# A mixture-of-experts loop whose blocks are pipelined by one: the down matmuls of a block between the gate-and-up chunks of the next

## The chip, the cores and the metric

The kernel runs on one core of a Trainium2 chip (trn2). The metric is the device time of one execution in microseconds. Times of before are of three runs and one profiled execution.

## The reference, cut to what matters

One step of an encoder layer on 336 tokens (64 of a sample stream, 272 of a prompt stream), all in fp32: norm and input projection, an mLSTM branch, a latent-attention branch, output projection, then a top-4-of-32 mixture of experts with clamped SwiGLU, and a final norm. The change touches the mixture of experts alone:

```python
logits = (x2 @ w_router) + b_router
top_v, top_i = lax.top_k(logits, 4)
gates = softmax(top_v)
...
def expert_block(xb, e):
    gu = xb @ w_gu[e] + b_gu[e]            # 1024 x 2048
    gate = minimum(gu[:, :1024], 7.0)
    up = clip(gu[:, 1024:], -7.0, 7.0)
    hid = (up + 1.0) * gate * sigmoid(1.702 * gate)
    return hid @ w_dn[e] + b_dn[e]         # 1024 x 1024
...
y[token] += expert_block(x2[token], e) * gate
```

## The kernel before, in words

The kernel is one program with an instruction stream written out by hand for each engine (sync, tensor, scalar, vector, gpsimd); engines meet at semaphores, and each stream runs in its own order. A long first part computes the mixing branches and the router. The change lies behind it, in the expert loop.

**Blocks.** Each token goes to four experts. The 1344 token rows are sorted by expert and padded to blocks of 64 rows (`BLK`). Every expert has at least one block. The number of blocks, `nb`, is read from a table at run time, as are the expert of each block (`bei`) and, for each expert, the last block of the expert before it (`firsti`). GpSimd scatters the normed rows into a DRAM buffer `x_rows` by an indirect DMA, and gathers the results from `y_rows` afterwards.

**Weights.** An expert has 8 MB of gate-and-up weights and 4 MB of down weights. The SBUF buffer `ring` has six slots of 2 MB: chunks 0 to 3 hold gate-and-up (two of eight contraction tiles each, `up_w`), chunks 4 and 5 hold down (`dn_w(0)`, `dn_w(1)`). Each chunk has one slot, so chunk c of an expert is loaded into the slot that the same chunk of the expert before has left. SyncE issues these loads in one stream:

```python
with sp.Fori(1, NE) as e:
    before = sp.value_load(firsti[...e...])
    for c in range(4):
        sp.wait_ge(m_up, before * 4 + c + 1)
        sp.dma_start(up_w(c), ...).then_inc(chunk_in[c], 16)
    for c in range(2):
        sp.wait_ge(m_down, before * 2 + c + 1)
        sp.dma_start(dn_w(c), ...).then_inc(chunk_in[4 + c], 16)
```

The waits are on the last block of the expert before. Lines 473 to 482; the change leaves them as they are. Chunks of expert 0 are loaded ahead of the loop.

**One block on TensorE** (lines 809 to 854): four bias matmuls (line 817) with a selection matrix `pick`; gate-and-up chunks 0 to 2 (line 826) and chunk 3 (line 834), gate half first, then up half; the eight turnings (transposes, line 502 by the helper `turn`) of the next block's token rows, `tokens_turned`; the four turnings of the hidden rows; the down matmuls in two halves (line 851). Bias and gate-and-up accumulate in banks 2 and 3, turned rows stand in banks 0 and 1, down in bank 4. The two column halves of a matmul go to two halves of the array's columns, so matmuls stand in pairs.

**Beside it.** VectorE clamps gate and up out of the banks (lines 1422, 1425; helper line 1112), makes `pick` for the next block, and multiplies (1428, 1430). ScalarE applies the sigmoid (1070), copies the turned tokens to `xg` (1072), the turned hidden rows to `hidT` (1074) and the result to `yrow` (1077); copies show as line 878. GpSimd loads the next block's rows into the one buffer `xrow` (1517), stores `yrow` in two halves (1521) and waits for the stores before it goes on (1522).

Of the kernel before, what the change touches and what calls it, by code (L numbers as in the profile page):

```python
# [15 lines left out]
F32 = mybir.dt.float32  # L16
# [6 lines left out]
D = 1024  # L23
# [133 lines left out]
def build(nc, i, o, x_rows_dram, y_rows_dram):  # L157
    with ExitStack() as ctx:
# [3 lines left out]
        def sem(name):  # L162
            return ctx.enter_context(nc.semaphore(name))
# [156 lines left out]
        def taken(eng, *name):  # L320
# [21 lines left out]
             "m_dve", "m_pick", "m_turn", "m_hidT", "fin_v", "fin_ss", "fin_s", "fin_out", "all_out"))  # L342
        m_rows_in = sem("m_rows_in")
        desti_set, blocks_out, x_sent = sem("desti_set"), sem("blocks_out"), sem("x_sent")
# [141 lines left out]
        def _(pe):  # L486
# [321 lines left out]
            tokens_turned()  # L808
            with pe.Fori(0, nb) as b:
                e = pe.value_load(bei[0:1, bass.ds(b, 1)].bitcast(I32), min_val=0, max_val=NE - 1)  # L810

                def half(bank, t):
                    return bank[BLK * t:BLK * t + BLK, :]

                pe.wait_ge(m_pick, b + 1)
                for q in range(4):
                    pe.matmul(half(gate_bank if q < 2 else up_bank, q % 2), pick[:, q, :], bgu[:, :],  # L817
                              start=True, stop=False, skip_group_check=True)
                pe.wait_ge(m_xg, b + 1)
                for c in range(4):  # L820
                    pe.wait_ge(chunk_in[c], 16 * e + 16)
                    w = up_w(c)
                    if c < 3:
                        for k in range(2):
                            for q in range(4):
                                ins = pe.matmul(half(gate_bank if q < 2 else up_bank, q % 2), xg[:, 2 * c + k, :],  # L826
                                                w[:, k, 512 * q:512 * q + 512], start=False, stop=False,
                                                skip_group_check=True)
                        ins.then_inc(m_up, 1)
                    else:  # L830
                        for bank_, q0, done in ((gate_bank, 0, m_gate), (up_bank, 2, m_up)):
                            for k in range(2):
                                for t in range(2):
                                    ins = pe.matmul(half(bank_, t), xg[:, 2 * c + k, :],  # L834
                                                    w[:, k, 512 * (q0 + t):512 * (q0 + t) + 512], start=False,
                                                    stop=(k == 1), skip_group_check=True)
                            ins.then_inc(done, 1)
                pe.wait_ge(m_xrow, 16 * b + 32)
                pe.sem_inc(m_rows_in, 1)
                tokens_turned()  # L840
                pe.wait_ge(m_hid, b + 1)
                for j in range(4):
                    ins = turn(ht_bank[:, 128 * j:128 * j + 128], hid[:, 128 * j:128 * j + 128])
                ins.then_inc(m_turn, 1)
                pe.wait_ge(m_hidT, b + 1)
                for c in range(2):
                    pe.wait_ge(chunk_in[4 + c], 16 * e + 16)
                    w = dn_w(c)
                    for j in range(4):
                        for t in range(2):  # L850
                            ins = pe.matmul(half(out_bank, t), hidT[:, j, BLK * c:BLK * c + BLK],  # L851
                                            w[:, j, 512 * t:512 * t + 512], start=(c == 0 and j == 0),
                                            stop=(c == 1 and j == 3), skip_group_check=True)
                    ins.then_inc(m_down, 1)


        @block.scalar
        def _(act):
# [208 lines left out]
            signal(tokens(), m_xg, 1)  # L1067
            with act.Fori(0, nb) as b:
                act.wait_ge(m_gt, b + 1)
                act.activation(sg, gt, ACT.Sigmoid, scale=ALPHA).then_inc(m_sig, 1)  # L1070
                act.wait_ge(m_gath, b + 2)
                tokens().then_inc(m_xg, 1)
                act.wait_ge(m_turn, b + 1)
                copy(hidT[:, :, :], banks[1][:, :].rearrange("p (j s) -> p j s", j=4)).then_inc(m_hidT, 1)
                act.wait_ge(m_down, 2 * b + 2)
                act.wait_ge(yrow_free, b + 1)
                copy(yrow, banks[4][:, :]).then_inc(m_yrow, 1)
                act.wait_ge(m_yrow, b + 1)
                act.wait_ge(moe_tab, 1)
                act.nop()  # L1080


# [9 lines left out]
        def _(dve):  # L1092
# [327 lines left out]
            with dve.Fori(0, nb) as b:  # L1420
                dve.wait_ge(m_gate, b + 1)
                ts(gt, banks[2][:, :], LIMIT, ALU.min).then_inc(m_gt, 1)
                ts(pick[:, :, :], lane, be[:, bass.ds(dve.snap(b + 1), 1)], ALU.is_equal).then_inc(m_pick, 1)
                dve.wait_ge(m_up, 4 * b + 4)
                ts(up, banks[3][:, :], LIMIT, ALU.min, -LIMIT, ALU.max).then_inc(m_dve, 1)
                dve.wait_ge(m_sig, b + 1)
                dve.wait_ge(m_gt, b + 1)
                tt(gt, gt, sg, ALU.mult).then_inc(m_dve, 1)
                dve.wait_ge(m_dve, 2 * b + 2)
                stt(hid, up, 1.0, gt, ALU.add, ALU.mult).then_inc(m_hid, 1)  # L1430
                dve.wait_ge(m_hid, b + 1)
                dve.wait_ge(m_pick, b + 2)
                dve.wait_ge(moe_tab, 1)
                dve.nop()
# [20 lines left out]
        def _(pool):  # L1455
# [10 lines left out]
            for n in range(16):  # L1466
                b0, b1 = (MAXB + 1) * n // 16, (MAXB + 1) * (n + 1) // 16
                pool.dma_start(x_rows_dram[b0 * BLK:b1 * BLK, :].rearrange("(b s) d -> s b d", s=BLK),
# [43 lines left out]
            pool.sem_inc(yrow_free, 1)  # L1512
            with pool.Fori(0, nb) as b:
                src = x_rows_dram[bass.ds(pool.snap(b * BLK + BLK), BLK), :]
                dst = y_rows_dram[bass.ds(pool.snap(b * BLK), BLK), :]
                pool.wait_ge(m_gath, b + 1)
                pool.dma_start(xrow, src).then_inc(m_xrow, 16)
                pool.wait_ge(m_yrow, b + 1)
                pool.wait_ge(moe_tab, 1)
                for h in range(2):  # L1520
                    pool.dma_start(dst[:, 512 * h:512 * h + 512], yrow[BLK * h:BLK * h + BLK, :]).then_inc(m_store, 16)  # L1521
                pool.wait_ge(m_store, 32 * b + 32)
                pool.sem_inc(yrow_free, 1)
            pool.wait_ge(m_store, 32 * nb)
            pool.wait_ge(m_xrow, 16 * nb + 16)
            word = u_pad[0:1, 0, 67:68]
# [50 lines left out]
```

## Time and profile before

| | us |
|---|---|
| median of 3 runs (lowest to highest) | 2060.36 (2055.08 to 2061.68) |
| profiled execution, own time | 2061.79 |
| its span, first to last instruction | 2060.2 |
| TensorE matmul busy | 1719.9 (83%) |
| VectorE, ScalarE, GpSimd busy | 372.7, 337.3, 117.5 |
| mean granted TensorE clock | 0.887 of full speed |

Spans and starts are counted from the profile's first instruction; each engine's busy time is the union of its instructions. "PE" is TensorE, "DVE" VectorE, "ACT" ScalarE, "POOL" GpSimd, "SP" SyncE; a q behind an engine is its sequencer. A timeline merges like instructions in a row: start, us, engine, line, operation, output and inputs, how many, and in brackets the idle time before them with what ended it. A matmul of an fp32 operand stands as two instructions, so a chunk of 8 matmuls shows as x16.

### The profile page before, as it was taken

Reading aid. Unit: us, or ns where it says so; the run is one execution under the profiler, and the core shown is the slowest. Engines: PE = TensorE matmul, PEld = TensorE weight load, DVE = VectorE, ACT = ScalarE, POOL = GpSimd, SP = SyncE. Lnnn points to the kernel's source line nnn. Section 1 sums busy time; section 2 is a strip of 40 time slices with the busy share of each in tenths; the row PEclk is TensorE's granted clock in tenths of the full one; section 3 lists DMA queues with packets and bytes.
Section 4 is the critical chain, followed back from the end, with each engine's and each line's share of the span. In section 5 each row is a group of like instructions: output and inputs, shape, how many; then the busy total and the mean of one; then the engine's idle time right before and its main releaser. Section 6 shows DMA issues by size and latency. Waiting matters only on the chain.

```text
span 2060.2 us, 19415 instructions
## 1 busy us (share of the span) xinstructions
PE 1719.9 (83%) x7088; PEld 789.1 (38%) x7089; DVE 372.7 (18%) x899; ACT 337.3 (16%) x695; POOL 117.5 (6%) x219
## 2 busy tenths in 40 slices
PE   3999978688889998589877999979799987899890
PEld 1666544355556663333222333323233322233330
DVE  1371143322220011511010111101110111011113
ACT  1141254211221000111110111101111110111111
POOL 0021000000000000200000000000000000000003
PEclk9999976766669999599999999998999999999995
DMA  9396200110013344399999879999977999759894
GB/s 306 118 256 196 102 21 0 34 39 2 1 41 123 113 169 156 141 367 405 408 405 402 317 272 403 405 403 413 401 297 267 412 402 399 290 209 403 315 365 137
DMA packets 112324, 510.75 MB, mean 248 GB/s; under 512 B 8513, under 2 KB 12334, under 8 KB 79390
## 3 DMA queue, kind: packets, MB, share of 16 engines
q1 hardware_dynamic: 95790, 454.97, 56.4%
q0 software_dynamic: 16496, 55.29, 9.2%
q8 instruction: 22, 0.36, 0.1%
q14 instruction: 16, 0.13, 0.0%
HBM read 470.95 MB, written 39.28 MB: 248 GB/s over the span
## 4 chain that ended last, share of the span: by engine, by line
PE 65%; DMA 22%; DVE 6%; ACT 3%; issue 3%; SPq 1%; POOL 0%; DVEq 0%; POOLq 0%; ACTq 0%
PE bank L498 31%; DMA ring<-in_w_gate_up 18%; PE bank L826 12%; PE bank L851 10%; PE bank L834 7%; PE bank L502 2%; PE bank L817 2%; DVE r_c L1118 1%; DMA ring<-in_w_down 1%; ACT ring L878 1%; DMA ring<-in_w_in 1%; DVE r_v L1118 1%; DVE r_kv L1115 1%; ACT r_kv L878 1%; DMA y_rows<-r_xt 0%
## 5 line engine op out<-in xcount | busy, mean ns | idle before, releaser
L826 PE MATMUL bank<-ring,r_kv 128*64 128x512 f32 x1872 | 412.9, 593 | 27.2 <-DMA ring<-in_w_gate_up 27.2
L851 PE MATMUL bank<-ring,r_kv 128*64 128x512 f32 x1248 | 315.0, 662 | 27.8 <-ACT r_kv L878 26.8
L498 PE MATMUL bank<-r_xt,ring 128*128 128x336 f32 (+2 forms) x896 | 259.8, 453 | 8.6 <-DMA ring<-in_w_in 8.6
L826 PEld LDWEIGHTS bank<-ring,r_kv 128*64 128x64 f32 x1872 | 131.2, 137 | 302.6 <-issue 253.4
L1112 DVE TENSOR_SCALAR r_kv<-bank 128x512 f32<-128x512 f32 (+1 forms) x80 | 55.0, 687 | 1038.0 <-PE bank L834 1016.2
L498 PEld LDWEIGHTS bank<-r_xt,ring 128*128 128x128 f32 (+2 forms) x896 | 167.5, 188 | 99.1 <-issue 20.4
L834 PE MATMUL bank<-ring,r_kv 128*64 128x512 f32 x624 | 151.3, 630 | 39.9 <-DMA ring<-in_w_gate_up 39.9
L851 PEld LDWEIGHTS bank<-ring,r_kv 128*64 128x64 f32 x1248 | 94.7, 153 | 223.2 <-issue 181.5
L1070 ACT ACTIVATE r_o<-r_kv 128x512 f32<-128x512 f32 x39 | 24.6, 630 | 562.2 <-DVE r_kv L1112 562.2
L502 PE MATMUL bank<-const,r_v 64*128 64x64 f32 (+3 forms) x524 | 62.9, 258 | 60.0 <-DVE r_v L1118 49.3
L834 PEld LDWEIGHTS bank<-ring,r_kv 128*64 128x64 f32 x624 | 45.5, 144 | 141.6 <-issue 88.4
L498 PE MATMUL bank<-ring 64*128 64x257 f32 (+4 forms) x208 | 78.6, 526 | 22.4 <-DVE r_qk L1115 11.1
L1521 POOL DMA_DIRECT2D y_rows<-r_xt x78 | 41.8, 536 | 855.0 <-ACT r_xt L878 833.7
L502 PEld LDWEIGHTS bank<-const,r_v 64*128 64x128 f32 (+3 forms) x524 | 46.2, 140 | 100.2 <-DVE r_v L1118 54.5
L878 ACT ACTIVATE r_xt<-bank 128x512 f32<-128x512 f32 x39 | 23.3, 597 | 320.0 <-PE bank L851 320.0
L817 PE MATMUL bank<-bgu,r_qk 128*64 128x512 f32 x312 | 74.8, 601 | 0.0
L498 PE MATMUL bank<-r_kv,ring 128*128 128x336 f32 (+10 forms) x240 | 73.8, 448 | 0.0
L878 ACT ACTIVATE r_kv<-bank 128x512 f32<-128x512 f32 (+3 forms) x85 | 49.8, 586 | 134.8 <-PE bank L502 134.6
L498 PEld LDWEIGHTS bank<-ring 64*128 64x128 f32 (+4 forms) x208 | 42.9, 223 | 52.5 <-issue 34.0
L498 PEld LDWEIGHTS bank<-r_kv,ring 128*128 128x128 f32 (+3 forms) x240 | 44.7, 225 | 26.1 <-issue 15.5
L498 PE MATMUL bank<-ring,r_kv 128*128 128x128 f32 (+4 forms) x160 | 49.1, 453 | 6.4 <-ACT ring L878 6.4
L1070 ACT ACT_TABLE_LOAD x39 | 50.0, 1283 | 12.7 <-ACT r_xt L878 12.6
(212 smaller groups left out, 1092.7 us busy)
## 6 DMA issues: line engine op xcount, KB each, us to landing
ring<-in_w_gate_up SPq DMA_DIRECT2D x128, 2048.0 KB, 20.6
ring<-in_w_down SPq DMA_DIRECT2D x64, 2048.0 KB, 21.4
ring<-in_w_in SPq DMA_DIRECT2D x12, 2048.0 KB, 7.8
r_v<-x_rows POOLq DMA_DIRECT2D x40, 256.0 KB, 7.3
y_rows<-r_xt POOLq DMA_DIRECT2D x78, 128.0 KB, 5.5
x_rows<-r_c POOLq DMA_DIRECT2D x10, 768.0 KB, 18.4
x_rows<-r_c POOLq DMA_DIRECT2D x6, 1024.0 KB, 21.6
y_rows<-r_c POOLq DMA_DIRECT2D x1, 5376.0 KB, 33.1
```

Of the source, the lines that this page charges most:

```text
L498: ins = pe.matmul(out, l, r, start=(n == 0), stop=(n == len(pairs) - 1), **kw)
L502: return pe.transpose(out, src, ident[0:src.shape[0], 0:src.shape[0]])
L817: pe.matmul(half(gate_bank if q < 2 else up_bank, q % 2), pick[:, q, :], bgu[:, :], start=True, stop=False, skip_group_check=True)
L826: ins = pe.matmul(half(gate_bank if q < 2 else up_bank, q % 2), xg[:, 2 * c + k, :], w[:, k, 512 * q:512 * q + 512], start=False, stop=Fal ...
L834: ins = pe.matmul(half(bank_, t), xg[:, 2 * c + k, :], w[:, k, 512 * (q0 + t):512 * (q0 + t) + 512], start=False, stop=(k == 1), skip_grou ...
L851: ins = pe.matmul(half(out_bank, t), hidT[:, j, BLK * c:BLK * c + BLK], w[:, j, 512 * t:512 * t + 512], start=(c == 0 and j == 0), stop=(c ...
L878: return act.activation(out, src, ACT.Copy, scale=scale)
L1070: act.activation(sg, gt, ACT.Sigmoid, scale=ALPHA).then_inc(m_sig, 1)
L1112: return dve.tensor_scalar(out, a, s1, s2, op0, op1)
L1115: return dve.tensor_tensor(out, a, b, op)
L1118: return dve.scalar_tensor_tensor(out=out, in0=a, scalar=s, in1=b, op0=op0, op1=op1)
L1521: pool.dma_start(dst[:, 512 * h:512 * h + 512], yrow[BLK * h:BLK * h + BLK, :]).then_inc(m_store, 16)
```

## The change

The TensorE stream is cut into `bias`, `gate_up`, `hidden_turned` and `down`. Block 0's bias and gate-and-up run ahead of the loop; each iteration then does bias and chunk 0 of block b, the hidden turning of block b-1, chunk 1, the down matmuls of block b-1, chunks 2 and 3 and the turning of the next token rows; the last block's down stands behind the loop. A new semaphore `m_read` says that the up half has been read, and the bias of the next block waits for it. `down` waits for `yrow_free`, where the ScalarE copy did before. ScalarE's hidden and result copies move by one block to the head of its iteration. GpSimd issues the row load of block b+2 in iteration b, behind the stores of block b-1, and `x_rows` gets one more zeroed block. The body of `gate_up` is the old one, indented otherwise, as is that of `half`.

```diff
-        m_rows_in = sem("m_rows_in")
+        m_rows_in, m_read = sem("m_rows_in"), sem("m_read")
...
@@ -806,43 +806,48 @@
-            with pe.Fori(0, nb) as b:
-                e = pe.value_load(bei[0:1, bass.ds(b, 1)].bitcast(I32), min_val=0, max_val=NE - 1)
...
+            def bias(b):
 
                 pe.wait_ge(m_pick, b + 1)
                 for q in range(4):
                     pe.matmul(half(gate_bank if q < 2 else up_bank, q % 2), pick[:, q, :], bgu[:, :],
                               start=True, stop=False, skip_group_check=True)
-                pe.wait_ge(m_xg, b + 1)
-                for c in range(4):
-                    pe.wait_ge(chunk_in[c], 16 * e + 16)
-                    w = up_w(c)
-                    if c < 3:
+
+            def gate_up(c, e):
+
+                pe.wait_ge(chunk_in[c], 16 * e + 16)
+                w = up_w(c)
+                if c < 3:
...
-                pe.wait_ge(m_xrow, 16 * b + 32)
-                pe.sem_inc(m_rows_in, 1)
-                tokens_turned()
...
+            def hidden_turned(b):
+
                 pe.wait_ge(m_hid, b + 1)
                 for j in range(4):
                     ins = turn(ht_bank[:, 128 * j:128 * j + 128], hid[:, 128 * j:128 * j + 128])
                 ins.then_inc(m_turn, 1)
+
+            def down(b, e):
+
                 pe.wait_ge(m_hidT, b + 1)
+                pe.wait_ge(yrow_free, b + 1)
...
+            bias(0)
+            pe.wait_ge(m_xg, 1)
+            for c in range(4):
+                gate_up(c, 0)
+            pe.wait_ge(m_xrow, 32)
+            tokens_turned()
+            with pe.Fori(1, nb) as b:
+                e = pe.value_load(bei[0:1, bass.ds(b, 1)].bitcast(I32), min_val=0, max_val=NE - 1)
+                before = pe.value_load(bei[0:1, bass.ds(pe.snap(b - 1), 1)].bitcast(I32), min_val=0, max_val=NE - 1)
+                pe.wait_ge(m_read, b)
+                bias(b)
+                pe.wait_ge(m_xg, b + 1)
+                gate_up(0, e)
+                hidden_turned(b - 1)
+                gate_up(1, e)
+                down(b - 1, before)
+                gate_up(2, e)
+                gate_up(3, e)
+                pe.wait_ge(m_xrow, 16 * b + 32)
+                pe.sem_inc(m_rows_in, 1)
+                tokens_turned()
+            hidden_turned(nb - 1)
+            down(nb - 1, NE - 1)
...
@@ -1065,19 +1094,30 @@
-            with act.Fori(0, nb) as b:
+
+            def hidden_out(b):
+                act.wait_ge(m_turn, b + 1)
+                copy(hidT[:, :, :], banks[1][:, :].rearrange("p (j s) -> p j s", j=4)).then_inc(m_hidT, 1)
+
+            def rows_out(b):
+                act.wait_ge(m_down, 2 * b + 2)
+                copy(yrow, banks[4][:, :]).then_inc(m_yrow, 1)
+
+            act.wait_ge(m_gt, 1)
+            act.activation(sg, gt, ACT.Sigmoid, scale=ALPHA).then_inc(m_sig, 1)
+            act.wait_ge(m_gath, 2)
+            tokens().then_inc(m_xg, 1)
+            with act.Fori(1, nb) as b:
+                hidden_out(b - 1)
+                rows_out(b - 1)
                 act.wait_ge(m_gt, b + 1)
                 act.activation(sg, gt, ACT.Sigmoid, scale=ALPHA).then_inc(m_sig, 1)
                 act.wait_ge(m_gath, b + 2)
                 tokens().then_inc(m_xg, 1)
-                act.wait_ge(m_turn, b + 1)
-                copy(hidT[:, :, :], banks[1][:, :].rearrange("p (j s) -> p j s", j=4)).then_inc(m_hidT, 1)
-                act.wait_ge(m_down, 2 * b + 2)
-                act.wait_ge(yrow_free, b + 1)
-                copy(yrow, banks[4][:, :]).then_inc(m_yrow, 1)
-                act.wait_ge(m_yrow, b + 1)
                 act.wait_ge(moe_tab, 1)
                 act.nop()
+            hidden_out(nb - 1)
+            rows_out(nb - 1)
...
@@ -1422,11 +1462,12 @@
-                ts(up, banks[3][:, :], LIMIT, ALU.min, -LIMIT, ALU.max).then_inc(m_dve, 1)
+                ts(up, banks[3][:, :], LIMIT, ALU.min, -LIMIT, ALU.max).then_inc(m_read, 1)
...
-                dve.wait_ge(m_dve, 2 * b + 2)
+                dve.wait_ge(m_read, b + 1)
+                dve.wait_ge(m_dve, b + 1)
...
@@ -1464,7 +1505,7 @@
-                b0, b1 = (MAXB + 1) * n // 16, (MAXB + 1) * (n + 1) // 16
+                b0, b1 = (MAXB + 2) * n // 16, (MAXB + 2) * (n + 1) // 16
...
@@ -1510,19 +1551,27 @@
-            with pool.Fori(0, nb) as b:
-                src = x_rows_dram[bass.ds(pool.snap(b * BLK + BLK), BLK), :]
-                dst = y_rows_dram[bass.ds(pool.snap(b * BLK), BLK), :]
-                pool.wait_ge(m_gath, b + 1)
-                pool.dma_start(xrow, src).then_inc(m_xrow, 16)
-                pool.wait_ge(m_yrow, b + 1)
+            pool.wait_ge(m_gath, 1)
+            pool.dma_start(xrow, x_rows_dram[BLK:2 * BLK, :]).then_inc(m_xrow, 16)
+            pool.wait_ge(m_gath, 2)
+            pool.dma_start(xrow, x_rows_dram[2 * BLK:3 * BLK, :]).then_inc(m_xrow, 16)
+            with pool.Fori(1, nb) as b:
+                src = x_rows_dram[bass.ds(pool.snap(b * BLK + 2 * BLK), BLK), :]
+                dst = y_rows_dram[bass.ds(pool.snap(b * BLK - BLK), BLK), :]
+                pool.wait_ge(m_yrow, b)
                 pool.wait_ge(moe_tab, 1)
                 for h in range(2):
                     pool.dma_start(dst[:, 512 * h:512 * h + 512], yrow[BLK * h:BLK * h + BLK, :]).then_inc(m_store, 16)
-                pool.wait_ge(m_store, 32 * b + 32)
+                pool.wait_ge(m_gath, b + 2)
+                pool.dma_start(xrow, src).then_inc(m_xrow, 16)
+                pool.wait_ge(m_store, 32 * b)
                 pool.sem_inc(yrow_free, 1)
+            dst = y_rows_dram[bass.ds(pool.snap(nb * BLK - BLK), BLK), :]
+            pool.wait_ge(m_yrow, nb)
+            for h in range(2):
+                pool.dma_start(dst[:, 512 * h:512 * h + 512], yrow[BLK * h:BLK * h + BLK, :]).then_inc(m_store, 16)
             pool.wait_ge(m_store, 32 * nb)
-            pool.wait_ge(m_xrow, 16 * nb + 16)
+            pool.wait_ge(m_xrow, 16 * nb + 32)
             word = u_pad[0:1, 0, 67:68]
             pool.tensor_tensor(word, word, word, ALU.add).then_inc(blocks_out, 1)
```

The order of TensorE's instructions in the loop body, as the compiled programs have it. `m_xg` is the copy of turned tokens, `m_hid` and `m_hidT` the hidden rows and their turned copy, `chunk_in0` to `chunk_in5` the landed weights. Before, from the bias to the end of the down matmuls:

```order
L817 MATMUL bank<-bgu,r_qk 64x512 [waits m_pick]
L821 ISA [waits m_xg]
L826 MATMUL bank<-ring,r_kv 64x512 [waits chunk_in0]
L826 MATMUL bank<-ring,r_kv 64x512 [waits chunk_in1]
L826 MATMUL bank<-ring,r_kv 64x512 [waits chunk_in2]
L834 MATMUL bank<-ring,r_kv 64x512 [waits chunk_in3]
L502 MATMUL bank<-const,r_v 128x64 [waits m_xrow]
L502 MATMUL bank<-const,r_v 128x128 [waits m_hid]
L851 MATMUL bank<-ring,r_kv 64x512 [waits chunk_in4,m_hidT]
L851 MATMUL bank<-ring,r_kv 64x512 [waits chunk_in5]
```

And of the change, where lines 827 and 835 are the gate-and-up matmuls and 856 the down matmuls:

```order
L815 REGISTER_ALU [waits m_read]
L817 MATMUL bank<-bgu,r_qk 64x512 [waits m_pick]
L827 MATMUL bank<-ring,r_kv 64x512 [waits chunk_in0]
L502 MATMUL bank<-const,r_v 128x128 [waits m_hid]
L827 MATMUL bank<-ring,r_kv 64x512 [waits chunk_in1]
L852 ISA [waits yrow_free,m_hidT]
L856 MATMUL bank<-ring,r_kv 64x512 [waits chunk_in4]
L856 MATMUL bank<-ring,r_kv 64x512 [waits chunk_in5]
L827 MATMUL bank<-ring,r_kv 64x512 [waits chunk_in2]
L835 MATMUL bank<-ring,r_kv 64x512 [waits chunk_in3]
L502 MATMUL bank<-const,r_v 128x64 [waits m_xrow]
```

The waits for chunks 4 and 5 now stand between those for chunks 1 and 2, and belong to the block before; chunk 0's matmuls stand between the end of a block and its hidden turning.

SyncE's weight loads, the same in both programs: one expert's part of the loop.

```order
L477 DMA ring<-in_w_gate_up 128x2x2048
L476 REGISTER_ALU
L477 ISA [waits m_up]
L477 DMA ring<-in_w_gate_up 128x2x2048
L480 ISA
L481 ISA [waits m_down]
L481 DMA ring<-in_w_down 128x4x1024
L480 REGISTER_ALU
L481 ISA [waits m_down]
L481 DMA ring<-in_w_down 128x4x1024
```

The last gate-and-up chunks and then both down chunks stand in one stream, with the next expert's chunk 0 behind them; nothing moved here, while the order of TensorE's signals did.

## Rows read from the trace of the kernel before

**Rows 1.** The page: its span and the DMA rate in 40 equal slices.

```profile
span 2060.2 us, 19415 instructions
...
GB/s 306 118 256 196 102 21 0 34 39 2 1 41 123 113 169 156 141 367 405 408 405 402 317 272 403 405 403 413 401 297 267 412 402 399 290 209 403 315 365 137
```

**Rows 2.** The page, its chain that ended last, by line.

```profile
PE bank L498 31%; DMA ring<-in_w_gate_up 18%; PE bank L826 12%; PE bank L851 10%; PE bank L834 7%; PE bank L502 2%; PE bank L817 2%; DVE r_c L1118 1%; DMA ring<-in_w_down 1%; ACT ring L878 1%; DMA ring<-in_w_in 1%; DVE r_v L1118 1%; DVE r_kv L1115 1%; ACT r_kv L878 1%; DMA y_rows<-r_xt 0%
```

**Rows 3.** Windows of the expert loop: busy us, granted clock, DMA share, GB/s.

```profile
1144.50:1337.10 192.60, 177.39 (x816) 60.19 (x814) 20.52 (x35) 25.93 (x35) 11.21 (x21) 0.94 0.91 356
1337.10:1500.10 163.00, 129.87 (x584) 42.45 (x582) 14.66 (x25) 18.52 (x25) 8.02 (x15) 0.95 0.98 390
...
870.90:2012.10 1141.20, 988.03 (x4525) 332.45 (x4524) 114.37 (x195) 144.47 (x195) 61.41 (x115) 0.95 0.91 360
```

**Rows 4.** Waits of TensorE in the expert loop: us in total, times, longest.

```profile
PE bank L834 <- DMA ring<-in_w_gate_up: 39.9, 14, 3.3
PE bank L826 <- DMA ring<-in_w_gate_up: 27.2, 21, 1.7
...
PE bank L502 <- DMA r_v<-x_rows: 8.9, 13, 2.4
```

**Rows 5.** Timeline of TensorE, a block in which no weights are late.

```profile
1144.51 1.89 PE L817 MATMUL bank<-bgu,r_qk 128*64 128x512 f32 x8
1146.23 10.47 PE L826 MATMUL bank<-ring,r_kv 128*64 128x512 f32 x48
1156.53 3.60 PE L834 MATMUL bank<-ring,r_kv 128*64 128x512 f32 x16
1160.07 0.71 PE L502 MATMUL bank<-const,r_v 64*128 64x64 f32 x8
1162.25 0.65 PE L502 MATMUL bank<-const,r_v 128*128 128x128 f32 x4 [1.48 <-DVE r_v L1118]
1163.59 8.70 PE L851 MATMUL bank<-ring,r_kv 128*64 128x512 f32 x32 [0.69 <-ACT r_kv L878]
1172.12 1.88 PE L817 MATMUL bank<-bgu,r_qk 128*64 128x512 f32 x8
```

**Rows 6.** Timeline of TensorE, blocks in which it waits for weights.

```profile
1091.35 3.65 PE L826 MATMUL bank<-ring,r_kv 128*64 128x512 f32 x16 [1.72 <-DMA ring<-in_w_gate_up]
1097.98 5.35 PE L834 MATMUL bank<-ring,r_kv 128*64 128x512 f32 x16 [2.97 <-DMA ring<-in_w_gate_up]
...
1106.79 7.09 PE L851 MATMUL bank<-ring,r_kv 128*64 128x512 f32 x32 [0.69 <-ACT r_kv L878]
...
1123.73 3.65 PE L826 MATMUL bank<-ring,r_kv 128*64 128x512 f32 x16 [1.28 <-DMA ring<-in_w_gate_up]
1130.48 3.65 PE L834 MATMUL bank<-ring,r_kv 128*64 128x512 f32 x16 [3.09 <-DMA ring<-in_w_gate_up]
```

**Rows 7.** Timeline of SyncE's issues, some experts (start us, us).

```profile
1150.03 10.66 SPq L477 DMA_DIRECT2D ring<-in_w_gate_up  x4
...
1177.63 10.66 SPq L477 DMA_DIRECT2D ring<-in_w_gate_up  x4
...
1232.47 7.22 SPq L477 DMA_DIRECT2D ring<-in_w_gate_up  x3
```

**Rows 8.** The page: activations of the gate, one in each block.

```profile
L1070 ACT ACTIVATE r_o<-r_kv 128x512 f32<-128x512 f32 x39 | 24.6, 630 | 562.2 <-DVE r_kv L1112 562.2
```

**Rows 9.** The page, its DMA issues: KB each, median us to landing.

```profile
ring<-in_w_in SPq DMA_DIRECT2D x12, 2048.0 KB, 7.8
r_v<-x_rows POOLq DMA_DIRECT2D x40, 256.0 KB, 7.3
```

**Rows 10.** Gate-and-up weights: landing times, 878 to 1110, then 1144 to 1240 us.

```profile
DMA to landing us min/median/max: 8.0/24.7/28.3
...
DMA to landing us min/median/max: 8.8/12.4/18.5
```

**Rows 11.** Timeline of VectorE at the end of a block.

```profile
1160.18 0.69 DVE L1112 TENSOR_SCALAR r_kv<-bank 128x512 f32<-128x512 f32 x1 [0.76 <-PE bank L834]
```

More of the change, by code:

```diff
@@ L808, in _, with half @@
             tokens_turned()
-            with pe.Fori(0, nb) as b:
-                e = pe.value_load(bei[0:1, bass.ds(b, 1)].bitcast(I32), min_val=0, max_val=NE - 1)
-                def half(bank, t):
-                    return bank[BLK * t:BLK * t + BLK, :]
+            def half(bank, t):
+                return bank[BLK * t:BLK * t + BLK, :]
+            def bias(b):
                 pe.wait_ge(m_pick, b + 1)
@@ L818, in _ @@
                               start=True, stop=False, skip_group_check=True)
-                pe.wait_ge(m_xg, b + 1)
-                for c in range(4):
-                    pe.wait_ge(chunk_in[c], 16 * e + 16)
-                    w = up_w(c)
-                    if c < 3:
-                        for k in range(2):
[L825 to L837, printed above, removed]
@@ L838, in _ @@
-                pe.wait_ge(m_xrow, 16 * b + 32)
-                pe.sem_inc(m_rows_in, 1)
-                tokens_turned()
+            def gate_up(c, e):
+                pe.wait_ge(chunk_in[c], 16 * e + 16)
+                w = up_w(c)
+                if c < 3:
+                    for k in range(2):
+                        for q in range(4):
+                            ins = pe.matmul(half(gate_bank if q < 2 else up_bank, q % 2), xg[:, 2 * c + k, :],
+                                            w[:, k, 512 * q:512 * q + 512], start=False, stop=False,
+                                            skip_group_check=True)
+                    ins.then_inc(m_up, 1)
+                else:
+                    for bank_, q0, done in ((gate_bank, 0, m_gate), (up_bank, 2, m_up)):
+                        for k in range(2):
+                            for t in range(2):
+                                ins = pe.matmul(half(bank_, t), xg[:, 2 * c + k, :],
+                                                w[:, k, 512 * (q0 + t):512 * (q0 + t) + 512], start=False,
+                                                stop=(k == 1), skip_group_check=True)
+                        ins.then_inc(done, 1)
@@ L1571 @@
         o[name] = nc.dram_tensor("out_" + name, shape, F32, kind="ExternalOutput").ap()
-    x_rows_dram = nc.dram_tensor("x_rows", ((MAXB + 1) * BLK, D), F32).ap()
+    x_rows_dram = nc.dram_tensor("x_rows", ((MAXB + 2) * BLK, D), F32).ap()
     y_rows_dram = nc.dram_tensor("y_rows", (MAXB * BLK, D), F32).ap()
```

## The prediction

> **What bounds the kernel now.** I read the page first: the span is 2060.2 us, and from about slice 17 on the DMA engines move some 405 GB/s, with dips to 209 to 317 in a few slices [rows 1]. The chain gives weight DMAs of the experts 18% and the three matmul lines of the expert loop 12, 10 and 7% [rows 2], so neither side bounds alone. The windows of the loop put it at 1141.2 us, from the first bias matmul at 870.9 to the last copy out at 2012.1; TensorE is busy 988 of them, and the stretches differ: one at 356 GB/s with TensorE busy 177.4 of 192.6 us, one at 390 GB/s with it busy 129.9 of 163.0 [rows 3]. TensorE's waits for gate-and-up weights sum to only 67 us, those for token rows to 8.9 [rows 4]. There are thus two regimes.
>
> Where no weights are late, a block takes 27.6 us from bias to bias [rows 5]: bias 1.7, gate-and-up 13.8, tokens turned 0.7, a pause for the activation, hidden turned 0.7, another pause, and the down matmuls in 8.5 to 8.7 us. In the other regime the same chunk comes 32.4 us after that of the expert before (1123.73 less 1091.35; 1130.48 less 1097.98), and there the down matmuls take 7.09 [rows 6]. That is the rate of the DMA engines: six chunks of 2048 KB and 512 KB of token rows and results are 13.1 MB, which at 405 GB/s take 32.4 us. One chunk is 5.2 us, the rows of a block 1.3.
>
> What joins the regimes is the number of blocks: 39 activations of the gate [rows 8], 32 experts, so 7 extra blocks. SyncE's issues show where: the usual step from expert to expert is about 27.6 us and a two-block expert shows as 54.8 [rows 7]; over the loop six experts stand out so, one with three blocks. During an extra block the next expert's chunks find no free slot, and afterwards TensorE works off stored chunks for several blocks at 27.4.
>
> **The change, part by part.**
>
> TensorE's own work. Down matmuls no longer follow a pause. A block is bias 1.7, two chunks of 3.45, hidden turned 0.7, down 6.9 (1113.7 less 1106.8 at the warm clock), two more chunks, tokens turned 0.7 [rows 5, 6]: 23.8 us. At the block's end the new wait for the read of the up half holds the bias: VectorE reads until 1160.87, the tokens are turned by 1160.78 [rows 5, 11], so 0.1 plus the hand-over, 0.3 in all (0 to 1.5, since loop instructions stand there too). 24.1 us a block, 39 of them 940 us. The waits for hidden and its copy go: both are ready some 3 us after the block's end, and bias and chunk 0 are 5.2 us long. The last block still shows them, and the first bias runs slow: 4 us together. The new wait for the result buffer costs nothing: the store is issued a microsecond after the down matmuls, and the next down comes 17 us later. The row load is issued right after the turning instead of behind the last store, lands in 7.3 us [rows 9] and has 24; the 8.9 us of row waits go. It is no deeper in blocks, since the one buffer stays. The one more zeroed block is 256 KB in a stage at some 100 to 200 GB/s [rows 1]. POOL now stores before it loads, and both finish early; ScalarE loses a table load a block, off the path.
>
> The weights' order. SyncE's instructions are unchanged, and it waits in order: chunks 0 to 3 of an expert, then down chunks 4 and 5, then chunk 0 of the next. Before, consumption had the same order. Now the down matmuls of block b come after chunk 1 of block b+1, so chunk 4 can be asked for only then, and chunks 0 and 1 of the following expert, whose slots are already free, stand behind it in SyncE's stream. The stored lead is gone. With one-block experts the loop is closed: chunk 1 lands, its matmuls 3.45, the first half of down and the issue 3.8 (1150.03 less 1146.23 is matmul start to issue [rows 5, 7]), landing of chunk 4 after 8.0 [rows 10], chunks 5, 0 and 1 at 5.2 and the rows 1.3: 32.1 us. The DMA engines' own 32.4 is the floor, so 32.4 a block, and 8.3 of it TensorE waits for chunk 0. It escapes that wait only in extra blocks, and in the first block of an expert after them, whose chunks 0 and 1 were asked for early. Of 39 blocks, experts 2 to 31 have a first block, less 6 that follow a longer expert: 24 waits, 199 us.
>
> Without the clock the sum is 940 + 4 + 199 = 1143 us, where now there are 1141: the faster blocks are given back, since each expert alone takes the DMA time and each extra block adds 24.1 less 8.3.
>
> The landing of 8.0 us is the least seen in the loop, with a drained queue; an earlier like load has 7.8 [rows 9], and in the later window the least is 8.8 [rows 10]. From 7.8 the floor holds; 8.8 makes the loop 32.9, or 12 us more in all. I take 8.0, because chunk 3 is still moving when chunk 4 is issued.
>
> The Trainium skill ("DMA: Bandwidth & Descriptors", the anatomy of one DMA) gives a DMA a fixed cost of about 2.0 us beside its bytes. By it a landing would be 7.2 and the closed loop 31.3, still under the floor; the trace has 8.0, which decides.
>
> The clock. A wait of 3.0 us for chunk 3 is followed by matmuls of 5.35 us instead of 3.65 [rows 6], and the pauses before down by 8.7 instead of 7.09 [rows 5, 6]: granted half clock, 1.6 to 1.7 us lost. The new wait of 8.3 us is longer than any in the rows, so chunk 0 will start at 1.2 GHz in each of the 24 blocks. At most all its matmuls run so, and 3.5 are lost. Between the landings of chunk 0 and 1 there are 5.2 us, the warm work in it is 4.1 with the hidden turned: 1.1 are free. A loss of 1.7 delays the loop by 0.6, one of 3.5 by 2.4; one under 1.1 by nothing. I take a loss of 1.9, nearest to the rows, and 0.8 of delay: 24 x 0.8 = 19 us.
>
> Sum: 1143 + 19 - 1141 = 21 us slower. The profiled execution took 2061.79 us, 1.4 over the median of three; from the median, 2081.
>
> **The rivals.** (A) Not slower: the clock's loss stays in the slack between chunks 0 and 1, landings are 8.0 or less, and the floor of 32.4 rules. For it: 1.1 us of slack against rows of 1.7, close. Then +2 us, 2062; it decides if the matmuls of chunk 0 take under 4.6 us. It is as far as the gain can go unless the engines themselves get faster. (B) Cold and late: chunk 0 is wholly at half clock, 2.4 us a block, and landings are 8.8, 0.5: 24 x 2.9 = 70, with the 2 above +72, 2132. For it: the wait is more than twice the 3.0 that costs 1.7 already; against: the pauses before down lost 1.6 of a possible 7. The Trainium skill ("TensorE: Matmul & The Clock Gate", HAM oscillation) says that a loop which waits for a DMA in every tile starts each one throttled and loses half of the throttled time; it speaks for the forecast and for B over A, and the 3.0 us wait above agrees with it. (C) Faster: row loads and stores fall beside chunk landings and cost nothing: the block is then six chunks at 5.2, 31.2, and 24 x 1.2 = 29 us less than A: 2033. Against it: the engines' share is 0.98 in a stretch at 390 GB/s [rows 3], so there is no gap to fall into. (D) Not what it says: chunks 4 and 5 get issued early enough that the old lead stays. The one stream on SyncE excludes it.
>
> **How the numbers follow.** Chances: forecast (delays between 0.2 and 1.8 us a block, 2067 to 2106) 0.58, A 0.20, B 0.16, C 0.06. A measurement of this kernel tells 0.3% from no change, 6 us: faster ends at 2054, slower begins at 2067. So faster 0.06, same 0.20, slower 0.74. The range reaches from just under A, 2055, to 2117, which takes in a delay of 1.8 with landings of 8.8, and leaves out all of C and most of B.
>
> **What would show it.** In the timeline of TensorE nearly every one-block expert has one wait of about 8 us before chunk 0 and none before chunks 2, 3 or a down chunk; weight waits rise from 67 to about 200 us; the down matmuls start straight after chunk 1 and take 7 us; two blocks of a longer expert follow at 24 us. Chunk 0 after the wait takes about 5.5 us. SyncE issues both down chunks and chunks 0 and 1 in one burst. The median landing of gate-and-up chunks falls well below 20.6. I am wrong if waits before chunk 0 are absent, if the step between one-block experts is under 32, or if TensorE waits for down chunks, the result buffer or token rows.

## The result, and the profile after

| | before | changed |
|---|---|---|
| median | 2059.39 us of 4 runs (2055.08 to 2061.68) | 2113.47 us of 4 runs (2109.45 to 2115.21) |
| profiled execution's span | 2060.2 | 2113.3 |
| expert loop, first bias matmul to last copy out | 1141.8 | 1196.0 |
| mean granted TensorE clock | 0.887 | 0.873 |

The ratio of the times is 1.026, with a 95% interval of 1.024 to 1.029. The kernel is slower by 54 us, in the forecast direction and by two and a half times the 21 us forecast; 2113 lies inside the stated range and outside the forecast's own band of 2067 to 2106. The expert loop is 54 us longer, so the whole difference lies in it.

The page of the changed kernel, its span, the DMA rate in 40 slices and the landing times (answering to [rows 1]; before, 20.6 us was the median landing of gate-and-up chunks, 21.4 that of down chunks):

```profile
span 2113.3 us, 19546 instructions
...
GB/s 305 131 251 191 80 21 0 33 40 0 40 40 120 116 202 92 261 361 386 372 386 350 324 334 331 384 375 392 349 313 327 332 389 382 264 244 393 293 338 134
...
ring<-in_w_gate_up SPq DMA_DIRECT2D x128, 2048.0 KB, 20.1
...
ring<-in_w_down SPq DMA_DIRECT2D x64, 2048.0 KB, 10.3
```

The plateau at 405 GB/s is gone: in the slices of the loop the engines now reach 393 at most. Down chunks land in half the time, because few transfers stand ahead of them.

The waits of TensorE in the loop (answering to [rows 4]), and the loop as one window: us, busy us of TensorE, weight loads, VectorE, ScalarE, GpSimd, granted clock, DMA share, GB/s (answering to [rows 3]):

```profile
PE bank L827 <- DMA ring<-in_w_gate_up: 197.7, 24, 8.9
PE bank L817 <- DVE r_kv L1152: 8.9, 38, 0.2
PE bank L502 <- DVE r_v L1158: 1.6, 1, 1.6
PE bank L856 <- ACT r_kv L907: 0.7, 1, 0.7
```

```profile
870.00:2066.00 1196.00, 986.69 (x4527) 333.47 (x4526) 114.54 (x195) 96.01 (x158) 61.76 (x116) 0.92 0.90 343
```

There are 24 waits for weights, all before chunk 0, of 8.2 us in the mean; the new wait for the read of the up half costs 0.2 us a block, and the waits for token rows are gone. TensorE's busy time in the loop is 986.7 us, where it was 988.0.

The timeline of TensorE, one step between one-block experts and then a block without a wait (answering to [rows 5, 6]):

```profile
1095.68 5.05 PE L827 MATMUL bank<-ring,r_kv 128*64 128x512 f32 x16 [8.80 <-DMA ring<-in_w_gate_up]
1100.67 0.65 PE L502 MATMUL bank<-const,r_v 128*128 128x128 f32 x4
1101.25 3.65 PE L827 MATMUL bank<-ring,r_kv 128*64 128x512 f32 x16
1104.74 7.04 PE L856 MATMUL bank<-ring,r_kv 128*64 128x512 f32 x32
...
1119.51 1.94 PE L817 MATMUL bank<-bgu,r_qk 128*64 128x512 f32 x8 [0.23 <-DVE r_kv L1152]
1129.46 5.23 PE L827 MATMUL bank<-ring,r_kv 128*64 128x512 f32 x16 [8.01 <-DMA ring<-in_w_gate_up]
...
1153.47 1.94 PE L817 MATMUL bank<-bgu,r_qk 128*64 128x512 f32 x8 [0.23 <-DVE r_kv L1152]
1155.23 3.61 PE L827 MATMUL bank<-ring,r_kv 128*64 128x512 f32 x16
...
1177.62 1.94 PE L817 MATMUL bank<-bgu,r_qk 128*64 128x512 f32 x8 [0.23 <-DVE r_kv L1152]
```

A block without a wait takes 24.15 us (1177.62 less 1153.47). From one landing of chunk 0 to the next, 1095.68 to 1129.46, it is 33.8; over the 23 steps between bias matmuls that hold a wait the mean is 34.5 us, where the prediction had 33.2. The down matmuls follow chunk 1 without a pause and take 7.04.

SyncE's issues in this step, and the landing times of its two down chunks and four gate-and-up chunks (window 1100 to 1130):

```profile
1108.52 3.80 SPq L481 DMA_DIRECT2D ring<-in_w_down  x2
1113.60 5.58 SPq L477 DMA_DIRECT2D ring<-in_w_gate_up  x4
```

```profile
DMA to landing us min/median/max: 7.8/9.3/10.8
...
DMA to landing us min/median/max: 15.8/22.0/25.5
```

This is the closed loop in full. Chunk 0 lands at 1095.6, chunk 1's matmuls begin at 1101.25 (5.6), down at 1104.74 (3.5), chunk 4 is asked for at 1108.52 (3.8) and lands 7.8 later, at 1116.3; chunk 5, asked for at 1111.9, lands after 10.8, at 1122.7, and chunk 0, asked for at 1113.6 though its slot came free at 1100.7, after 15.8, at 1129.4. The landings of chunks 5 and 0 are thus 6.4 and 6.7 us apart.

The same engines by windows (columns as above), while chunk 3 lands, then at the start of chunk 4, later in chunk 4, from chunk 4 to 5, and during the row load:

```profile
1100.00:1108.00 8.00, 8.00 (x40) 2.77 (x38) 0.00 (x0) 0.60 (x1) 0.00 (x0) 1.00 1.01 421
1109.00:1111.00 2.00, 2.00 (x12) 0.72 (x10) 0.00 (x0) 0.00 (x0) 0.00 (x0) 1.00 0.53 117
1111.00:1115.00 4.00, 4.00 (x20) 1.29 (x18) 0.00 (x0) 0.60 (x1) 1.07 (x2) 1.00 1.01 414
1115.20:1117.20 2.00, 2.00 (x13) 0.59 (x10) 0.23 (x1) 0.00 (x0) 0.00 (x0) 1.00 0.97 289
1123.50:1127.00 3.50, 0.00 (x0) 0.00 (x0) 0.00 (x0) 0.00 (x0) 0.00 (x0) 0.84 1.03 329
```

For 2 us the engines move 117 GB/s instead of 421: chunk 3, which lands at 1110.5, is out before chunk 4 has begun, 1.4 us of transfer time lost (2 x 304 / 421). Another patch at 289 GB/s follows where chunk 5 takes over. The last window, at 329 GB/s, is not of the restart: the row load was issued at 1119.99 and landed 8.2 us later, and the kernel before shows the same rate while its row load runs, with engines that were not dry (its row load landed at 1130.3):

```profile
1125.50:1129.00 3.50, 1.89 (x10) 0.43 (x6) 0.00 (x0) 0.00 (x0) 0.00 (x0) 1.00 1.01 328
```

### The profile page after: what moved, and what is told of

It reads as the page before. It is cut to its first block, busy times and chain, and to the rows that moved or that the text cites. A ratio compares the mean times of both kernels' runs of the same rounds, so it can differ in the third digit from the quotient of the medians.

```text
span 2113.3 us, 19546 instructions
## 1 busy us (share of the span) xinstructions
PE 1718.3 (81%) x7088; PEld 789.0 (37%) x7089; DVE 372.9 (18%) x899; ACT 288.2 (14%) x657; POOL 116.6 (6%) x220
## 4 chain that ended last, share of the span: by engine, by line
PE 67%; DMA 20%; DVE 4%; issue 3%; SPq 2%; ACT 2%; POOL 1%; DVEq 0%; ACTq 0%; POOLq 0%
PE bank L498 30%; DMA ring<-in_w_gate_up 18%; PE bank L827 18%; PE bank L856 13%; PE bank L502 3%; PE bank L835 2%; PE bank L817 1%; DVE r_c L1158 1%; ACT ring L907 1%; DMA ring<-in_w_in 1%; POOL x_rows L1546 1%; SPq L474 1%; SPq L481 0%; DVE r_kv L1152 0%; SPq L425 0%
## 5 line engine op out<-in xcount | busy, mean ns | idle before, releaser
L907 ACT ACTIVATE ring<-bank 128x256 f32<-128x256 f32 (+11 forms) x108 | 36.2, 335 | 94.7 <-PE bank L502 51.1
```

What stands on the lines that cost most here:

```text
L907: return act.activation(out, src, ACT.Copy, scale=scale)
```

## The experiments

**Theories.** The closed loop: SyncE can ask for chunk 4 only after the first half of down, and everything behind it in its stream waits too; the place of the down matmuls among the chunks sets the time. The first rival is the half clock after long waits; the second, the new waits and loop instructions. Step means below are of the block steps with a weight wait, from bias to bias, the loop from the first bias matmul to the last copy out. Ratios are to the kernel before as it was run beside each experiment (2062.2 us beside the first four, 2060.6 beside the last four, 2059.4 in the main result). The changed kernel was not run again beside them, so a difference to it is good to some 3 us.

**Down ahead of chunk 0.** Slots come free in the order of SyncE's stream.

```diff
                 bias(b)
-                pe.wait_ge(m_xg, b + 1)
-                gate_up(0, e)
                 hidden_turned(b - 1)
-                gate_up(1, e)
                 down(b - 1, before)
-                gate_up(2, e)
-                gate_up(3, e)
+                pe.wait_ge(m_xg, b + 1)
+                for c in range(4):
+                    gate_up(c, e)
```

> The down matmuls of block b-1 stand right behind the bias of block b, ahead of chunk 0, so the slots come free in the order in which SyncE asks for them. Theory (the closed loop through chunk 4's landing costs the time): the lead of six chunks is back, blocks without late weights take 24.8 us, single experts 32.3; the loop takes about 1110 us, 85 less than the changed kernel's 1196, and the whole 2025 us. Weight waits fall from 198 to about 120 us and stand before several chunks. Rival (the half clock after long waits costs the time): the weights come at the engines' rate either way, waits of 8 us stay, and no more than 35 us come back: 2080. Rival (the new waits for reads and the loop's added instructions cost it): within 10 us of the changed kernel.

Measured: 2029.48 us, 0.983 of before (0.980 to 0.987), the loop 1112. Its timeline in a stretch of one-block experts and then in one without late weights:

```profile
1112.82 3.65 PE L856 MATMUL bank<-ring,r_kv 128*64 128x512 f32 x16 [0.76 <-ACT r_kv L905]
1116.87 3.65 PE L856 MATMUL bank<-ring,r_kv 128*64 128x512 f32 x16 [0.39 <-DMA ring<-in_w_down]
1122.05 3.65 PE L827 MATMUL bank<-ring,r_kv 128*64 128x512 f32 x16 [1.53 <-DMA ring<-in_w_gate_up]
1127.44 3.65 PE L827 MATMUL bank<-ring,r_kv 128*64 128x512 f32 x16 [1.73 <-DMA ring<-in_w_gate_up]
...
1145.29 3.65 PE L856 MATMUL bank<-ring,r_kv 128*64 128x512 f32 x16 [0.76 <-ACT r_kv L905]
...
1167.98 1.94 PE L817 MATMUL bank<-bgu,r_qk 128*64 128x512 f32 x8 [0.24 <-DVE r_kv L1150]
...
1192.96 1.94 PE L817 MATMUL bank<-bgu,r_qk 128*64 128x512 f32 x8 [0.23 <-DVE r_kv L1150]
```

```profile
876.00:1988.00 1112.00, 961.35 (x4528) 319.71 (x4526) 114.47 (x195) 95.64 (x157) 61.93 (x116) 1.00 0.94 369
```

One-block experts take 32.5 us (1145.29 less 1112.82), the engines' rate, and TensorE waits a little before every chunk, never long. Its clock is full for the whole loop. A free block takes 25.0. The stored lead is back too: six steps, the first of the loop that wait and those behind a longer expert, take 25 to 27 us, where the change has 34 to 36. All of the loss of the change is gone by moving a call, and the pipelining shows its gain: this kernel is faster than both, 1.7% below before.

**Down after chunk 0.** `hidden_turned` and `down` around `gate_up(0, e)`:

```diff
                 bias(b)
+                hidden_turned(b - 1)
                 pe.wait_ge(m_xg, b + 1)
                 gate_up(0, e)
-                hidden_turned(b - 1)
-                gate_up(1, e)
                 down(b - 1, before)
+                gate_up(1, e)
```

> The down matmuls stand behind chunk 0 instead of chunk 1: one chunk earlier in the closed loop. Theory: chunk 4 is asked for some 5 us earlier, before chunk 3 has landed, so the DMA engines don't run dry and single experts take their 32.3 us instead of 34.4; 24 blocks save 2 us or a little more: the whole about 2060, between before and 2070. Rival (half clock): the wait before chunk 0 stays at 7 to 8 us and with it the loss; under 15 us saved, 2100.

Measured: 2047.96 us, 0.991 of before (0.988 to 0.995), 65 below the change; the expected bounds were missed low by 12. Steps with a wait are 31 to 33 us for the most part, the loop 1129. There are still 24 waits, and the clock is 0.93 in the loop, so a low clock does not by itself bring the loss.

```profile
PE bank L827 <- DMA ring<-in_w_gate_up: 135.4, 24, 9.7
```

**Down after chunk 2.**

```diff
                 gate_up(1, e)
-                down(b - 1, before)
                 gate_up(2, e)
+                down(b - 1, before)
                 gate_up(3, e)
```

> The down matmuls stand behind chunk 2 instead of chunk 1: one chunk later in the closed loop. Theory: chunk 4 is asked for 5 us later (chunk 2 lands 5.0 after chunk 1), single experts take 38 to 39.5 us: 24 x 4 to 5 = 96 to 120 us more, the whole 2210 to 2235. Rival (half clock): the waits are cold already, so the same time within 20 us: 2095 to 2135.

Measured: 2208.99 us, 1.072 of before (1.069 to 1.076), 96 above the change and 1 below the range of the theory. Steps with a wait are 37.6 to 39.0 us, and the wait before chunk 0 is 11 to 12:

```profile
1103.75 1.94 PE L817 MATMUL bank<-bgu,r_qk 128*64 128x512 f32 x8 [0.24 <-DVE r_kv L1152]
1117.17 6.56 PE L827 MATMUL bank<-ring,r_kv 128*64 128x512 f32 x16 [11.48 <-DMA ring<-in_w_gate_up]
```

In the order of the four places the time is 2029, 2048, 2113, 2209. One chunk further, once the floor is left behind, adds nearly 4 us a step (38.2 in the mean against 34.5). Both rivals are out as the main cause: all four kernels wait for the same reads and have the same loop instructions, and the half clock can't give 96 us between the last two (chunk 0's matmuls after the wait take 5.9 us in the mean of 24, against 5.5 in the change: 8 us).

**Down loads in a stream of their own.** SyncE's two down loads are dropped, and ScalarE issues them, for every block; TensorE waits for them by block:

```diff
+                e = act.value_load(bei[0:1, bass.ds(b, 1)]...)
                 hidden_out(b - 1)
+                for c in range(2):
+                    act.wait_ge(m_down, 2 * b + c - 1)
+                    act.dma_start(dn_w(c), dn[:, bass.ds(e, 1), ...]...).then_inc(chunk_in[4 + c], 16)
                 rows_out(b - 1)
```

> ScalarE issues the loads of down chunks, SyncE those of gate-and-up alone, in the changed kernel's TensorE order. ScalarE loads the down weights for every block, so 7 x 4 MB are loaded twice (7 x 10 us of DMA time). Theory (SyncE's one stream holds the free slots of chunks 0 and 1 back): with the streams apart the lead is back; single experts 32.3 us, at most 12 of the long waits left: the loop 1090 to 1120, the whole 2010 to 2040. If the loop through chunk 4 counts and not the order of SyncE's stream, chunk 4 is as late as now and the waits move from chunk 0 to the down matmuls: 2100 or more.

Measured: 2105.67 us, 1.021 of before (1.018 to 1.024). The theory's 2010 to 2040 was missed. The time and the move of the waits to the down matmuls are those of the other branch, but not by its reason, a chunk 4 as late as before: the wait before chunk 0 is gone, and one before the second half of down, for chunk 5, took its place. A piece of the chain, and the waits:

```profile
1101.32 25.73 DMA ring<-in_w_down
1127.04 0.04 issue
1127.09 5.13 PE bank L852 x16
```

```profile
PE bank L852 <- DMA ring<-in_w_down: 158.2, 29, 11.1
```

Chunk 5 takes 25.7 us to land, where it took 10.8 in the change: the gate-and-up chunks of SyncE's stream are asked for early now and share the engines with it, though chunk 5 is wanted first. One that SyncE asked for at 1104.75, after chunk 5 (1101.32), landed 16.5 us later, at 1121.2, and chunk 5 at 1127.0. The steps of this stretch are 31.2 us; over the loop the steps with a wait are 32.4 in the mean, shorter than the 34.5 of the change, but there are 28 of them instead of 23. The 29 MB loaded twice add to it: over the loop the engines' share is 0.94 at 371 GB/s against 0.90 at 343. So the order in SyncE's stream did hold the free slots back, but lifting it by a second queue gave next to nothing: the order of delivery is lost with it, and the double loads weren't hidden as I had assumed. The run does not separate these two costs.

Turning SyncE's own order round (chunks 0 and 1 of the next expert ahead of chunks 4 and 5) wasn't tried: an expert with three blocks needs its down weights before its last block has freed chunk 0, and would wait for ever.

**A warm wait.** 16 idle matmuls fill the wait, to take the clock out of the loop:

```diff
                 bias(b)
+                for q in range(16):
+                    pe.matmul(half(banks[5], q % 2), pick[:, q % 4, :], bgu[:, :], start=True, stop=True, ...)
                 pe.wait_ge(m_xg, b + 1)
```

> The changed kernel with 16 more matmuls a block (as many as a half of down, into a bank that is not read) between the bias and chunk 0: they fill some 7 us of the wait of about 8, so TensorE is warm when chunk 0 lands. To be read by block: if the half clock lengthens the closed loop as the prediction has it (0.8 us), chunk 0's matmuls take 3.65 us instead of 5.0 to 5.5, and single experts 33.3 us instead of 34.4; if it doesn't, they stay at 34.4. Blocks without a wait grow by 7 us each, 14 or 15 of them, so the whole is 2175 to 2200 by either.

Measured: 2181.53 us, one run.

```profile
1093.33 3.65 PE L827 MATMUL bank<-ring,r_kv 128*64 128x512 f32 x16 [0.96 <-DMA ring<-in_w_gate_up]
...
1118.32 7.04 PE L873 MATMUL bank<-bgu,r_qk 128*64 128x512 f32 x32
1126.34 1.94 PE L827 MATMUL bank<-ring,r_kv 128*64 128x512 f32 x8 [0.97 <-DMA ring<-in_w_gate_up]
```

Chunk 0 takes 3.65 us, and the step is 33.0 (1126.34 less 1093.33); the mean of 23 is 33.5, against 34.5 in the change. The clock's part is 1.0 us a step, near the 0.8 of the prediction; a single run, but the steps are compared inside the traces. Free blocks are 31.0 us, which is where the added time went.

**Stores doubled.** Each result row is stored a second time, to a buffer that is read by nobody:

```diff
                     pool.dma_start(dst[:, 512 * h:512 * h + 512], yrow[...]).then_inc(m_store, 16)
+                for h in range(2):
+                    pool.dma_start(dst2[:, 512 * h:512 * h + 512], yrow[...]).then_inc(m_store, 16)
...
-                pool.wait_ge(m_store, 32 * b)
+                pool.wait_ge(m_store, 64 * b)
```

> The changed kernel with every result row stored a second time, to a buffer that nobody reads: 256 KB more a block. If the transfers after chunk 4's landing are a serial part of the closed loop, each single expert takes 0.65 to 1.5 us more: 24 of them, 15 to 36 us, 2129 to 2150. If rows fall into time in which the DMA engines are idle (rival C of the prediction), the time stays within 5 us of 2113.

Measured: 2146.8 us, 33 above the change; steps with a wait 35.6 in the mean, 1.1 more, free blocks 24.1 as before. 256 KB more cost 1.1 us, where 0.65 is their time at 405 GB/s. They don't fall into a gap: rival C is out.

**The row load alone.** The kernel before, with the next row load issued right after the turning (block 0's load and stores are written out ahead of the loop, not shown):

```diff
                 pool.wait_ge(m_gath, b + 1)
                 pool.dma_start(xrow, src).then_inc(m_xrow, 16)
+                pool.wait_ge(m_store, 32 * b)
+                pool.sem_inc(yrow_free, 1)
                 pool.wait_ge(m_yrow, b + 1)
...
-                pool.wait_ge(m_store, 32 * b + 32)
-                pool.sem_inc(yrow_free, 1)
```

> The kernel before, with one part of the change alone: the load of the next token rows is issued right after the turning and no longer behind the waits for the last block's stores. The 13 waits for rows, 8.9 us, go, and what little of them is not hidden by late weights is the gain: 5 to 9 us less than before, 2053. If the rows matter by their place among the weights' transfers instead, up to 10 us more.

Measured: 2061.03 us, 1.000 of before (0.998 to 1.003). The gain of 5 to 9 us did not come, though the waits for rows went:

```profile
PE bank L502 <- DVE r_v L1118: 57.8, 39, 1.5
PE bank L826 <- DMA ring<-in_w_gate_up: 38.8, 17, 3.3
PE bank L851 <- ACT r_kv L878: 26.8, 39, 0.7
PE bank L834 <- DMA ring<-in_w_gate_up: 9.4, 8, 1.8
```

The 8.9 us of [rows 4] turned into 8.5 more of the wait for the hidden rows (49.3 us before the change): the turning of the tokens stood in that pause anyway, so it could be late by 1.5 us for nothing. The waits for gate-and-up weights fell too, from 67 to 48 us, and TensorE's busy time in the loop rose by 17, from 988.0 to 1004.8, at a granted clock of 0.93 instead of 0.95; which of the two followed from the other was not tested.

**Down split.** Chunk 4's half of down after chunk 0, chunk 5's after chunk 1:

```diff
-                gate_up(0, e)
                 hidden_turned(b - 1)
+                gate_up(0, e)
+                down(b - 1, before, (0,))
                 gate_up(1, e)
-                down(b - 1, before)
+                down(b - 1, before, (1,))
```

> The changed kernel with the down matmuls in two halves: chunk 4's behind chunk 0, chunk 5's behind chunk 1 as now. Only chunk 4 is asked for earlier. If the DMA engines' running dry before chunk 4 is the term that the prediction had too small, single experts take 32.3 to 32.6 us instead of 34.4 (24 x 2 = 48 us less): 2055 to 2070. If chunk 5's later landing or the half clock makes the difference, at least half of it stays: 2090 or more.

Measured: 2066.47 us, 1.002 of before (1.000 to 1.004), 47 below the change. Steps with a wait are 32.5 us in the mean. Only chunk 4 is asked for earlier, chunk 5 and those behind it as in the change. One step of it as a window, from one landing of chunk 0 to the next:

```profile
1083.10:1115.70 32.60, 26.93 (x116) 8.82 (x117) 2.93 (x5) 2.42 (x4) 1.60 (x3) 0.87 1.02 405
```

and the step of the changed kernel shown above:

```profile
1095.70:1129.40 33.70, 25.52 (x116) 8.55 (x116) 2.93 (x5) 2.42 (x4) 1.60 (x3) 0.91 0.98 379
```

The engines move 405 GB/s instead of 379: they no longer run dry, and the 2 us over the floor vanish, though the granted clock of this step is even lower. With that the loop is 1146 us, near the 1143 of the prediction's sum without the clock.

What it does not show is that the restart made the landings behind chunk 4 late. SyncE's issues in this step, then the landing times of its two down chunks and of the four gate-and-up chunks behind them:

```profile
1093.32 7.24 SPq L481 DMA_DIRECT2D ring<-in_w_down  x2
1101.82 5.60 SPq L477 DMA_DIRECT2D ring<-in_w_gate_up  x4
```

```profile
DMA to landing us min/median/max: 8.9/9.3/9.8
...
DMA to landing us min/median/max: 13.8/19.8/23.4
```

Chunk 4 lands at 1103.1 (9.8), chunk 5, asked for at 1100.2, at 1109.1 (8.9), chunk 0 at 1115.6 (13.8): 6.0 and 6.5 us apart, with engines that were kept full.

## Why the prediction was right or wrong

**The closed loop, its place and its count: right.** 24 waits before chunk 0 and none before chunks 2 to 5, as the text had it; free blocks 24.15 against 24.1; row waits gone; the read wait 0.2; the four places of down order the time as the mechanism says.

**The clock: right in size.** 0.8 us a step forecast, 1.0 shown by the warm wait. Chunk 0's matmuls after the wait take 5.5 us in the mean of 24 (5.0 to 6.7), so the loss of 1.9 was right; the slack was smaller, since chunks 0 and 1 land 5.0 us apart and not 5.2.

**What failed is the size of the loop's DMA part.** The step was "chunks 5, 0 and 1 at 5.2 and the rows 1.3" behind chunk 4's landing, 16.9 us. In the step shown above, chunks 5 and 0 came 6.4 and 6.7 us after the one before, and chunk 1 5.0 after that, 18.1; the mean over the 24 is 18.1 too. I had spread one average rate, 405 GB/s, over chunks and rows. A chunk with no rows beside it lands 5.0 us after the one before, so three have 15.0, and the rows took the other 3.1, not 1.3: 1.7 beside the row load, 1.4 beside the stores. The 1.7 is no matter of a dry queue. It is in the split of down, and it stood in [rows 6]: the matmuls that waited for chunks 2 and 3 began 6.6 and 6.75 us apart, with a row load between.

The restart has a smaller part. In the 18 steps of the split kernel whose chunk 4 was asked for in time, chunks 5, 0 and 1 came 6.0, 6.6 and 5.0 us apart, 17.6: 0.7 of the missing 1.2 us are there without a dry queue, and up to 0.5 is left for the slow patch behind one. The dry gap ahead of chunk 4 was in the sum already, as the landing of 8.0, and 8.0 is the measured mean. At the engines the 2 us of a step over their floor show as that gap and the patch, and both go when chunk 4 is asked for in time; but of the two only the patch was missing from the sum. No run takes the row traffic out of the changed kernel, so this division rests on the landings, and on the doubled stores, which cost 1.1 us a step instead of 0.65.

**A second fault goes with it: a floor is not a sum.** I had 32.1 for the loop, took the floor of 32.4 instead and put the clock's 0.8 on top, 33.2. In the closed loop every part adds: 32.1 and 1.2 of transfers and 1.0 of clock make 34.3, where 34.5 was measured. Only with chunk 4 early enough does the floor rule, and then the clock's loss is hidden: the split of down has cold starts in its waits and still 32.5.

**The sum in numbers.** The forecast was 940 + 4 + 24 x 9.1 = 1162. Measured: 24.15 x 39 = 942, 24 waits' excess at 34.5 less 24.15, 248, and 6 for the two ends, 1196. Of the 34 us missing, 24 x 1.3 = 31 are the step's length.

**The ranges.** I named landings of 8.8 as the open end of the DMA part. The landing of chunk 4 was 7.8 in this step and 8.0 in the mean, so the end was set at the wrong place: the two behind it were late. That 2113 still lies under 2117 is luck: the upper end was made of a clock delay of 1.8 us and landings of 8.8, where the means were 1.0 and 8.0.

**The rivals.** A (the floor rules, 2062) is what the split of down shows, 2066, but by another way than A's: the cold start stayed, and an earlier load hid it. B's 2132 was nearer to the result than the forecast, and its reasons were not what happened: chunk 0 took 5.5 us where B had it wholly cold at 7, and landings were short. C is out by the doubled stores.

**The row load**, which I took for a saving of up to 8.9 us in the changed kernel, would have brought nothing to the old one; in the sum it had no part.

## What to carry to other kernels

When consumption is reordered, compare the new order with the order in which the loads are asked for: a ring of slots holds its lead only as far as the two agree, and one issuing stream makes the latest free slot the gate for all behind it. Here the same pipelining with down ahead of chunk 0 gives 0.983 of before, and with down two chunks later 1.026. In a closed loop through a load, list what lands inside the loop and price each by the landings seen, small transfers apart from large ones; count the restart of a dry DMA queue and every cold start in full, and add them. A rate averaged over engines that are kept full gives only the floor. A second queue lifts the gate and loses the order of delivery.

## What the runs showed of the hardware that I had not expected

- A next chunk asked for only 2 us before the last one lands (1108.5 and 1110.5) comes too late to keep the engines busy: 117 GB/s in the 2 us around the restart (421 before it). A second patch, 289 GB/s at a share of 0.97, follows where chunk 5 takes over; in the split kernel, whose engines weren't dry, the same take-over (1102 to 1104) has 334.
- During a token row load of 256 KB the engines' share is 1.03 at 329 GB/s, and 1.01 at 328 in the kernel before: the weight chunk beside it lands 6.6 to 6.75 us after the last instead of 5.0, where 256 KB at 405 would be 0.65.
- Two queues, each with 2 MB transfers, share the engines and not by age: the chunk wanted first took 25.7 us, and a gate-and-up load asked for 3.4 us after it landed 5.8 us before it.
